# The tables of relative bias built on GpSimd, in two operations a limit and head, instead of on VectorE

## What is computed

```python
def t5_bucket(dist):
    max_exact = REL_BUCKETS // 2          # REL_BUCKETS = 32
    d = jnp.maximum(dist, 0)
    dl = jnp.maximum(d, max_exact).astype(jnp.float32)
    large = max_exact + (jnp.log(dl / max_exact) / math.log(REL_MAX_DIST / max_exact)
                         * (REL_BUCKETS - max_exact)).astype(jnp.int32)
    large = jnp.minimum(large, REL_BUCKETS - 1)
    return jnp.where(d < max_exact, d, large)
...
        bias = rel_bias[t5_bucket(pb[:, :, None] - p_sel)]
        s = (jnp.einsum('bthd,btkd->bthk', qb, k_sel).astype(jnp.float32) * scale
             + jnp.moveaxis(bias, -1, 2).astype(jnp.float32))
```

## Time and profile before

| | |
|---|---|
| median of 3 runs | 2115.94 us (2115.22 to 2116.03) |
| span of the profiled execution, first to last instruction | 2112.8 us |
| what lies around the span (median less span) | 3.1 us |
| PE busy | 1902.5 us, 90% |
| DVE busy | 1142.6 us, 54% |
| ACT busy | 667.5 us, 32% |
| POOL busy | 25.4 us, 1%, 50 instructions |

### The profile page before, as it was taken

One profiled execution on the slowest core, in us unless ns is written; L12 is line 12 of the kernel. 1 busy time (PEld: TensorE's weight loads), 2 busy tenths in 40 slices (PEclk: granted clock), 3 DMA queues, 4 the chain that ended last, 5 costly groups with the idle time before them and its releaser, 6 DMA issues.

```text
span 2112.8 us, 19184 instructions
## 1 busy us (share of the span) xinstructions
PE 1902.5 (90%) x6900; PEld 1142.6 (54%) x6900; DVE 1142.6 (54%) x2306; ACT 667.5 (32%) x1340; POOL 25.4 (1%) x50
## 2 busy tenths in 40 slices
PE   5999999889899998989998876868999979999997
PEld 2444444434434444445333453556777868888785
DVE  4376676731999888532862352464445444444412
ACT  1123235311132344112112232335455334434411
POOL 2000000000000000000000000000000000000000
PEclk9999999999999998999998978978999979999998
DMA  6121112021211110032302011002333313332220
GB/s 219 40 80 40 41 49 67 27 80 40 80 40 40 40 70 1 1 111 72 89 20 60 12 59 30 14 18 75 90 90 102 113 41 99 100 98 84 98 100 40
DMA packets 153006, 135.79 MB, mean 64 GB/s; under 512 B 12673, under 2 KB 126977, under 8 KB 152913
## 3 DMA queue, kind: packets, MB, share of 16 engines
q1 hardware_dynamic: 149504, 124.53, 19.4%
q0 software_dynamic: 3408, 10.04, 1.6%
HBM read 130.36 MB, written 4.19 MB: 64 GB/s over the span
## 4 chain that ended last, share of the span: by engine, by line
PE 74%; DVE 16%; ACT 6%; issue 3%; DMA 1%; SPq 0%; DVEq 0%; ACTq 0%
PE proj L1262 24%; PE proj L1242 21%; PE proj L1259 11%; DVE rel_bias L1881 3%; PE proj L1239 2%; PE attn_out L1415 2%; PE score L1435 2%; PE score L1372 2%; PE proj L1435 1%; PE attn_out L1435 1%; PE turned_probs L1401 1%; DVE E L1951 1%; PE proj L1268 1%; PE turned_probs L1435 1%; DVE index_and_shared L1874 1%
## 5 line engine op out<-in xcount | busy, mean ns | idle before, releaser
L1262 PE MATMUL proj<-hT,weights 128*128 128x512 f32 x1216 | 561.9, 614 | 20.5 <-DVE raw L2135 11.4
L1262 PEld LDWEIGHTS proj<-hT,weights 128*128 128x128 f32 x1216 | 232.1, 196 | 302.6 <-issue 278.3
L1881 DVE SCALAR_TENSOR_TENSOR rel_bias<-index_and_shared,bias_deltas,rel_bias 128x128 f32<-128x128 f32 (+3 forms) x480 | 232.7, 547 | 4.3
L1242 PE MATMUL proj<-hT_high,weights_high 128*128 128x512 f32 x544 | 218.6, 402 | 7.6 <-DVE hT_low L2160 6.0
L1242 PE MATMUL proj<-hT_high,weights_low 128*128 128x512 f32 x544 | 215.8, 397 | 0.0
L1242 PE MATMUL proj<-hT_low,weights_high 128*128 128x512 f32 x544 | 215.5, 396 | 0.0
L2151 DVE TENSOR_TENSOR weights_low<-weights,weights_high 128x1024 fp32r<-128x1024 f32 (+1 forms) x122 | 135.3, 1116 | 96.4 <-ACT weights_high L1705 96.4
L1259 PE MATMUL proj<-weights,hT 128*128 128x512 f32 (+1 forms) x384 | 151.7, 553 | 0.1
L1705 ACT ACTIVATE weights_high<-weights 128x1024 fp32r<-128x1024 f32 (+1 forms) x122 | 111.5, 961 | 74.3 <-DMA weights<-in_w_ffn_down 60.5
L1242 PEld LDWEIGHTS proj<-hT_high,weights_high 128*128 128x128 f32 x544 | 103.2, 190 | 41.5 <-issue 9.5
L1453 ACT ACTIVATE tg<-proj 128x512 f32<-128x512 f32 x66 | 39.5, 599 | 267.0 <-PE proj L1242 212.2
(11 more groups left out here) (388 smaller groups left out, 2567.3 us busy)
## 6 DMA issues: line engine op xcount, KB each, us to landing
weights<-in_w_in SPq DMA_DIRECT2D x15, 2048.0 KB, 8.5
weights<-in_w_in SPq DMA_DIRECT2D x38, 512.0 KB, 4.2
weights<-in_w_ffn_gate SPq DMA_DIRECT2D x22, 512.0 KB, 4.1
weights<-in_w_ffn_up SPq DMA_DIRECT2D x22, 512.0 KB, 5.3
weights<-in_w_ffn_down SPq DMA_DIRECT2D x11, 1024.0 KB, 4.9
weights<-in_w_in SPq DMA_DIRECT2D x9, 1024.0 KB, 5.8
weights<-in_w_out SPq DMA_DIRECT2D x4, 2048.0 KB, 10.7
weights<-in_w_out SPq DMA_DIRECT2D x4, 1024.0 KB, 5.1
```

What stands on the lines that cost most here:

```text
L1242: mm = nc.tensor.matmul(ps[:, :], w_[:, k, c0:c0 + P], x_[:, k, :], start=first, stop=last)
L1262: mm = nc.tensor.matmul(ps[0:gr["M"], :], w[:, k, c0:c0 + gr["M"]], x[:, k, :], start=first, stop=last)
L1881: ins = nc.vector.scalar_tensor_tensor(o, mk, d, o, ALU.mult, ALU.add)
```

## The change

The step `bias` leaves the common list, and with it leave the DVE operations of L1873, L1874, L1879 and L1881. A function `bias_tile(t)` on POOL builds the tables of one tile. It first makes the negative distance for the tile in `below[0]`. Then it goes through the 31 limits, and for each head makes the compare and the product with the head's difference in one two-stage operation with one tensor input (`term`, in `below[1]`), and adds that to the table in a second operation with two tensor inputs. For the first limit the second operation adds a column instead. Each operation waits for the one ahead of it. The tiles stand at four places in POOL's list: tiles 0 and 1 behind the lambda rows of layer 0, tile 2 behind those of layer 1, tile 3 behind the layer norm rows of layer 1, ahead of the spill.

```diff
-N_BIAS = 4 * NT * (REL_BUCKETS - 1)
+N_BIAS = 4 * NT
...
-        state["bias_due"] += BIAS_RATES.get(items[min(n, len(items) - 1)]["kind"], 2)
-        while state["bias_due"] >= 1:
-            state["bias_due"] -= 1
-            if state["bias"] < len(bias_steps) and not only_block1:
-                steps.append(("bias", bias_steps[state["bias"]]))
-                state["bias"] += 1
...
+            link_n = Count(bias_step)
+
+            def link(ins):
+
+                pool.wait_ge(bias_step, link_n.on(ins))
+
+            def bias_tile(t):
+
+                K = P * (t + 1)
+                dist, term = below[0][:, 0:K], below[1][:, 0:K]
+                link(nc.gpsimd.tensor_scalar(dist, pkb[:, 0:K], pq[:, t:t + 1], None, ALU.subtract))
+                for b in range(REL_BUCKETS - 1, 0, -1):
+                    for h in range(4):
+                        o, d = b_at(h, t), deltas[:, b, h:h + 1]
+                        if b == REL_BUCKETS - 1:
+                            link(nc.gpsimd.tensor_scalar(o, dist, float(-BUCKET_STARTS[b]), d, ALU.is_le, ALU.mult))
+                            link(nc.gpsimd.tensor_scalar(o, o, deltas[:, 0, h:h + 1], None, ALU.add))
+                            continue
+                        link(nc.gpsimd.tensor_scalar(term, dist, float(-BUCKET_STARTS[b]), d, ALU.is_le, ALU.mult))
+                        add = nc.gpsimd.tensor_tensor(o, o, term, ALU.add)
+                        if b == 1:
+                            add.then_inc(bias_done, 1)
+                            pool.wait_ge(bias_done, 4 * t + h + 1)
+                        else:
+                            link(add)
+
             for l in range(DEPTH):
...
+                if not only_block1:
+                    if l == 0:
+                        pool.wait_ge(bias_ready, 1)
+                    for t in ((0, 1), (2,))[l]:
+                        bias_tile(t)
...
             if not only_block1:
+                bias_tile(NT - 1)
                 pool.wait_ge(ln_done, n_ln)
...
-                elif op == "bias":
-                    t, b = arg
-                    K = P * (t + 1)
-                    k = NT_BIAS(t, b)
-                    mk = below[k % 2][:, 0:K]
-
-                    if k >= 1:
-                        dve.wait_ge(bias_done, 4 * k)
-                    link(nc.vector.tensor_scalar(starts[:, 0:1], pq[:, t:t + 1], float(-BUCKET_STARTS[b]), None, ALU.add))
-                    nc.vector.tensor_scalar(mk, pkb[:, 0:K], starts[:, 0:1], None, ALU.is_le).then_inc(bias_mask, 1)
-                    dve.wait_ge(bias_mask, k + 1)
-                    for h in range(4):
-                        o, d = b_at(h, t), deltas[:, b, h:h + 1]
-                        if b == REL_BUCKETS - 1:
-                            ins = nc.vector.tensor_scalar(o, mk, d, deltas[:, 0, h:h + 1], ALU.mult, ALU.add)
-                        else:
-                            ins = nc.vector.scalar_tensor_tensor(o, mk, d, o, ALU.mult, ALU.add)
-                        ins.then_inc(bias_done, 1)
...
+                        nc.vector.tensor_copy(pq, pos_i[:, :]).then_inc(bias_ready, 1)
```

9 lines of the change are left out of this document (2 added, 7 removed).

## The result

The changed kernel takes 2431.14 us in the median of 4 runs (2429.94 to 2432.72), the kernel before 2115.58 us beside it (2113.88 to 2116.03). The ratio is 1.149, with a 95% interval of 1.1475 to 1.1507. That is slower, as forecast, but by 316 us and not by 86, and outside the range of 2120 to 2300.

A forecast was written before the change was run, and what follows sets the result against it. PE was taken as the bound, busy 1902.5 of 2112.8 us. POOL's tile 3 ending at 1043 instead of 956.4 us adds 86.6, giving a 2199.4 us span and, with 3.1 more, 2202 us; range 2120 to 2300.

The forecast's parts named there:

- The place and the kind of wait: ACT waits at "ik" for POOL's tile 3, PE stands behind it; the end moves by 86.6 us and nothing behind changes.
- shift = T3 - 191 - g: Move of the kernel's end: T3 is tile 3 with delays, g the gain before POOL's release; 303 - 191 - 25.
- the cost of the one-input operation on POOL: In POOL's table building: 0.69 us at 512 columns, taken between 0.49 and 1.22 us; a pair 2.21 us.
- The delays in tile 3: From DVE's operations on SBUF alone holding POOL up in tile 3: 30 us, between bounds of 0 and 45.
- Rival 2: POOL so slow that layer norm rows of layer 0 are late too: shift +202 us, 2318 us; chance 0.14.
- The falsifiers that the prediction named: Include a 512-column pair under 1.5 or over 2.6 us, and L1752 of layer 0 waiting for the rows.
- The gain g: Time saved up to POOL's release for tile 3, by taking tables off DVE: 25 us; 40 us in all.
- The sharing of SBUF: DVE and POOL operations on SBUF hold each other up; DVE's waits halve the gain in layer 0, 8 of 16 us.
- rival 3: SBUF access exclusive for a whole operation: g about 10 us, tile 3 delayed 45, shift +117 us, 2233 us; chance 0.14.
- Rival 1: POOL nearly as fast as VectorE, a pair below 1.49 us: 2076 or 2084 us; chance 0.10 with mixtures.
- 4: ACT does not wait for the tables at "ik"; the prediction excluded it and gave no chance.
- 5: The two sides cancel, within 4 us of 2116, with tile 3 between 212 and 220 us; chance 0.04.

The follow-up runs named there:

- mask_product: Changed kernel with POOL's slow compare made once a limit as a mask, and the product done as product plus zero; 2253.07 us, ratio 1.0646 to before.
- rows_inside: Changed kernel with transfers of layer 0's layer norm rows and layer 1's lambda rows issued from inside tile 1, behind 14 limits; 2436.69 us, ratio 1.1504.
- half_tile3: Changed kernel with 15 of the 31 limits (60 pairs) left out of tile 3; 2230.17 us, ratio 1.0531 to before.
- no_tables: Changed kernel with the tables only filled with zeros by 16 POOL operations, all sums left out; 2088.13 us, ratio 0.9856 to before.
- forms_together: Small separate kernel: POOL runs 120 compares with product, then 120 two-tensor adds, while DVE runs four forms beside each; run once, its time not read.

## Why the prediction was wrong, point by point

**The place and the kind of wait: right.** ACT waits at "ik", PE waits 268.5 us behind it, the rest keeps its length, and the spill, now 358 us later than in the earlier trace rows, costs nothing beside that. The span grew by as much as "ik" moved (317.1 and 317.4 us). mask_product shows the two waits on which the formula shift = T3 - 191 - g rests, `soft1_done` ahead of tile 3 and POOL ahead of "ik". In the changed kernel the first of them is gone: POOL is never idle ahead of tile 3, so that the formula no longer holds there.

**The failed step: the cost of the one-input operation on POOL.** The prediction took "a row between the ends, L1916: 0.69 us at 512 columns", with the scan's 1.22 us as the upper bound. It is 2.05 us in the kernel and 2.00 alone, so even the bound failed: a scan on VectorE doesn't bound an operation on another engine. The two-input operation (1.30 against 1.22) and the link (0.08 to 0.10 against 0.15) were sized well. The prediction also priced "one-input" as if the form didn't matter. That 0.69 us is close to what product and sum take (0.62 to 0.70 us) is luck: it was read from a reduction on DVE.

**What followed from it.** Tile 3 costs 120 x 3.45 us and 16 us for its 9 others, 430 us with nothing beside it, where 273 were forecast: +157. Tiles 0 to 2 take 795 us where 568 were forecast with their delays; 134 of the 227 us are covered by POOL's idle time before `soft1_done`, so tile 3 starts 93 us late, at 832.6 instead of 740. The delays in tile 3 are 441 - 430 = 11 us instead of 30: -19. Together +231 us, which is the 317.4 measured less the 86.6 forecast.

**Rival 2, "so slow that the rows are late too".** It is what happened: it was to begin at 2.5 us a pair, and 3.45 was measured. It had 0.14, and only 2318 us, since 1.25 times was the worst case that was priced. It also added the lateness of the rows to the shift. With its own numbers that is right, for its tile 2 would end near 747 us and the release come at 777; mask_product, where POOL is idle ahead of tile 3, shows it (13.5 us of wait, 8.6 us less of g). rows_inside shows that it isn't so once POOL is never idle: without the 70.6 us wait the kernel takes 2436.69 us, no less. The two waits stand in the shadow of the same list, and half_tile3 shows that shortening the list counts, 3.35 us a pair. The falsifiers that the prediction named, a pair over 2.6 us and L1752's successor waiting for the rows, are both there.

**The gain g.** Measured in no_tables, without any POOL work: 19.3 us against 25, and 24.0 in all against 40 (some 30 by the medians). The first layer norm comes 5.0 us earlier (10 forecast), from there to the release it is 14.3 us (15 forecast), and behind the release 4.7 (15 forecast). It was the idle time of PE and the low clock that were overrated. In the stretch from 763.15 to 854.13 us the granted clock rises from 0.87 to 0.94, and PE goes through the same instructions in 82.7 us instead of 91.4: 8.7 us of the 15. But at its start PE had gained only 16.9 us where the release had gained 19.3, and ahead of "ik" 1.6 us are lost again, which leaves the 24.0. In the changed kernel g is worth nothing, since POOL isn't released by DVE.

**The sharing of SBUF, and rival 3.** Its price on POOL's side was overrated (11 us in tile 3). On DVE's side operations do grow longer: the 305 us taken from DVE made it only 248 us less busy, and beside POOL the 16 operations of L1775 go from 692 to 969 ns. But while DVE has no tables to build, little of that reaches the path. The first layer norm of layer 0 would stand at 479.13 - 70.6 = 408.5 us in the changed kernel without its wait for the rows, and it stands at 408.86 in no_tables. So no run shows the sharing to take half of the gain of layer 0, as the prediction had it; the gain itself is small, 5.0 us with no sharing at all. That g falls to 10.7 us in mask_product, the "about 10" of rival 3, is a coincidence: there the late rows of rival 2 take it. forms_together shows the rule of rival 3 to be true for one of POOL's two operations and not for the other. The Trainium skill, SBUF — State Buffer, § Who interferes with whom, calls the lock exclusive, with the whole instruction of either side blocking the other. The add agrees (0.29 to 1.31 us); the compare with product doesn't (0.29 to 0.36 and 0.41 us beside operations of 2.03 us). That DVE's reduction is never held, as the Trainium skill says there, agrees: 286 ns beside both.

**Rivals 1, 4 and 5.** None came near. ACT did wait for the tables at "ik" (272.0 us), and the two sides didn't cancel. Rival 1 needed a pair under 1.49 us. With the cheap form a pair is 0.74 + 1.31 + 0.18 = 2.23 us, and 2.75 with its share of the masks and limits.

## What to carry to other kernels

Before work goes to GpSimd, run its exact instruction forms there for a few microseconds: a bound taken from another engine's rows isn't a bound, and one form of similar arithmetic can be over twice as cheap (0.70 us for product and sum with a column, 1.56 for the product alone). Then look at the list it joins: once it is never idle from end to end, only its own length counts, and transfers that stand in it should be put between its operations. And ask how often VectorE will meet a two-tensor add on GpSimd: a shorter operation between the adds brought them closer together, and while VectorE built tables beside them that made the kernel 26 us slower.

## What the runs showed of the hardware

- GpSimd, 128x512 float32, one tensor input: copy 0.62 us, product and sum 0.62 (two constants) and 0.70 (with a column), a single product or compare 1.49, with a column 1.56, compare and product 1.92 to 2.00; two tensors added 1.26. VectorE needs 0.43 to 0.49 us for all the one-input forms and 0.69 us for the two tensors. Why the single product is slower than product and sum wasn't looked into further.
- The Trainium skill, GPSIMD Engine Reference, § 4.1, calls operations with one input roughly line-rate. That is near the truth here for the copy and for product and sum, at 1.4 to 1.5 times VectorE, and not for the others, at 3.2 to 4.5 times. The Trainium skill, GPSIMD Engine Reference, § 3.1, on the two-input add, by which the prediction worked out an estimate of 1.12 us, agrees within 0.14 us.
- An operation on GpSimd that waits for the one ahead begins 0.08 to 0.10 us behind its end, on the mean of the groups above.
- A two-tensor add of 1.26 us on GpSimd held the SBUF operations of VectorE for its whole length (128 columns: 0.29 to 1.31 us). That was so for the three elementwise forms tried, and not for the reduction. The compare with product held them by 0.06 to 0.2 us. The product with sum held VectorE's sums of 128 columns not at all (0.34 to 0.35 us within it). Other forms on GpSimd weren't looked at for this.
- DVE operations with one tensor in PSUM keep their length in the changed kernel: L1789, which reads "proj", takes 687 ns beside POOL and 688 before.
